# A 256-token model of two hybrid blocks on one core: seven of the 32 weight pieces of each first-block mixer have their low parts subtracted by GpSimd

## What is computed

```python
for l in range(DEPTH):                       # first block, DEPTH = 2
    h = rms_norm(x, ffn1_norm[l])
    x = x + 0.5 * swiglu(h, ffn1_w_gate[l], ffn1_w_up[l], ffn1_w_down[l])
    h = rms_norm(x, mix_norm[l])
    (na_q, ..., dl_v) = split_in_proj(h @ w_in[l])
    o_a = neighborhood_attention(...); o_b = diff_attention(...)
    o_c = gqa_axial_attention(...);    o_d = dilated_attention(...)
    x = x + jnp.concatenate([o_a, o_b, o_c, o_d], axis=-1) @ w_out[l]
    h = rms_norm(x, ffn2_norm[l])
    x = x + 0.5 * swiglu(h, ffn2_w_gate[l], ffn2_w_up[l], ffn2_w_down[l])
...
for l in range(DEPTH):                       # second block
    h = rmsnorm(x, g_mix_pre[l]) * (1.0 + scale_a) + shift_a
    y = hybrid_mixer(h, ...)
    x = x + gate_a * rmsnorm(y, g_mix_post[l])
    h = rmsnorm(x, g_ffn_pre[l]) * (1.0 + scale_f) + shift_f
    x = x + gate_f * rmsnorm(swiglu_2(h, w_gate_up[l], w_down[l]), g_ffn_post[l])
```

## Time and profile before

| what | value |
|---|---|
| median of 3 runs | 1707.03 us (1704.61 to 1708.94) |
| the profiled execution, its own time | 1706.23 us |
| its span, first to last instruction | 1704.4 us |
| TensorE busy | 1633.8 us (96%), 8104 matmuls |
| VectorE busy | 1194.8 us (70%), 1833 instructions |
| ScalarE busy | 932.1 us (55%), 1789 instructions |
| GpSimd busy | 92.0 us (5%), 155 instructions |
| VectorE `Wl<-raw,Wh` (L1644) | 316 of 1.204 us |
| VectorE `QTl<-raw,QTh` (L1644) | 178 of 1.208 us |

### The profile page before, as it was taken

How to read it: one execution, slowest core, us unless ns; L and a number is a source line. 1 busy time by engine, 2 the same in 40 slices (tenths; PEclk the granted TensorE clock), 3 DMA queues, 4 the chain that set the end, 5 groups by cost and what they waited for, 6 DMA issues and landing times.

```text
span 1704.4 us, 22248 instructions
## 1 busy us (share of the span) xinstructions
PE 1633.8 (96%) x8104; PEld 1354.8 (79%) x8104; DVE 1194.8 (70%) x1833; ACT 932.1 (55%) x1789; POOL 92.0 (5%) x155
## 2 busy tenths in 40 slices
PE   7999998899999999998899999989999989899998
PEld 6888877788888888877788887778788878778887
DVE  6877689777776777769787776767645476675554
ACT  6445568654445444557754445757534467664342
POOL 0000112100000000022000000101000010010000
PEclk9999999999999999999999999999999999999999
DMA  8787634277866887634177784523665642346551
GB/s 315 265 296 257 218 112 136 87 266 253 278 231 204 276 279 253 241 100 143 50 243 275 254 275 135 176 99 95 219 201 176 182 156 82 112 139 222 197 182 63
DMA packets 100107, 329.87 MB, mean 194 GB/s; under 512 B 18800, under 2 KB 19312, under 8 KB 99488
## 3 DMA queue, kind: packets, MB, share of 16 engines
q1 hardware_dynamic: 85504, 276.59, 48.4%
q10 hardware_dynamic: 14496, 51.87, 9.2%
HBM read 327.32 MB, written 1.10 MB: 193 GB/s over the span
## 4 chain that ended last, share of the span: by engine, by line
PE 45%; DVE 6%; ACT 3%; issue 1%; POOL 1%; DVEq 0%; POOLq 0%; ACTq 0%
PE PS L819 14%; PE PS L821 14%; PE PS L820 14%; PE PS L973 1%; PE PS L885 1%; DVE Wl L1644 1%; DVE PTl L1840 1%; PE PS L993 1%; DVE st L1809 1%; ACT WK L1368 1%; DVE QTl L1644 0%; DVE WK L1806 0%; PE PS L1150 0%; ACT Wh L1252 0%; ACT WK L1379 0%
## 5 line engine op out<-in xcount | busy, mean ns | idle before, releaser
L1644 DVE TENSOR_TENSOR Wl<-raw,Wh 128x1024 fp32r<-128x1024 f32 (+1 forms) x316 | 371.0, 1204 | 44.9 <-ACT Wh L1252 44.0
L819 PE MATMUL PS<-Wh,Hh 128*128 128x512 f32 (+2 forms) x936 | 370.2, 396 | 9.5 <-DVE Hl L1707 3.5
L820 PE MATMUL PS<-Wl,Hh 128*128 128x512 f32 (+2 forms) x936 | 365.0, 390 | 0.0
L821 PE MATMUL PS<-Wh,Hl 128*128 128x512 f32 (+2 forms) x936 | 364.9, 390 | 0.0
L1252 ACT ACTIVATE Wh<-raw 128x1024 fp32r<-128x1024 f32 (+1 forms) x316 | 317.4, 1041 | 25.8 <-DVE PTl L1755 11.0
L1644 DVE TENSOR_TENSOR QTl<-raw,QTh 128x1024 fp32r<-128x1024 f32 (+2 forms) x178 | 211.5, 1208 | 19.8 <-ACT QTh L1252 19.6
L819 PEld LDWEIGHTS PS<-Wh,Hh 128*128 128x128 f32 x936 | 178.2, 190 | 48.9 <-DVE WK L1740 3.9
L821 PEld LDWEIGHTS PS<-Wh,Hl 128*128 128x128 f32 x936 | 178.2, 190 | 36.4
L820 PEld LDWEIGHTS PS<-Wl,Hh 128*128 128x128 f32 x936 | 178.3, 191 | 33.9
L819 PE MATMUL PS<-QTh,Hh 128*128 128x512 f32 (+2 forms) x504 | 196.5, 390 | 3.8 <-DVE Hl L1707 3.8
L821 PE MATMUL PS<-QTh,Hl 128*128 128x512 f32 (+2 forms) x504 | 194.9, 387 | 0.0
(11 more groups left out here) (232 smaller groups left out, 2525.0 us busy)
## 6 DMA issues: line engine op xcount, KB each, us to landing
raw<-in_ffn SPq DMA_DIRECT2D x396, 512.0 KB, 5.3
BT<-in_ada ACTq DMA_DIRECT2D x96, 512.0 KB, 4.5
raw<-in_win SPq DMA_DIRECT2D x64, 512.0 KB, 4.5
raw<-in_wo SPq DMA_DIRECT2D x32, 512.0 KB, 4.5
...
```

The lines of the kernel that those rows point to most:

```text
L819: e.matmul(out_, xh, wh, start=start, stop=False)
L820: e.matmul(out_, xh, wl, start=False, stop=False)
L821: return e.matmul(out_, xl, wh, start=False, stop=stop)
L1644: ins = e.tensor_tensor(low(p)[:, 0:w], raw[p % RAW][:, 0:w], high(p)[:, 0:w].bitcast(f32), ALU.subtract)
```

## The change

GpSimd takes the low parts of pieces 10, 13, 16, 19, 22, 25 and 28 of each stage `a`; VectorE leaves them out. They are counted on a semaphore of their own, `w_low_pool`; `w_lo` counts the rest. Whoever waited for `w_lo` of a piece now calls `wait_low`. The events of both kinds of mixer are in a new order on TensorE, ScalarE and VectorE, and GpSimd's list of stage `a` has `parts` events. Second-block mixers have no piece on GpSimd; only their lists are changed.

```diff
+POOL_PIECES = (10, 13, 16, 19, 22, 25, 28)
...
             "PE": [("proj", 0, 0, 0), mid[0], mid[1], ("proj", 1, 0, 0), ("proj", 0, 1, 0), ("proj", 1, 1, 0),
                 ("proj", 2, 0, 0), ("turn_qk", 0, 0, 0), ("proj", 2, 1, 0), ("S", 0, 0, 0), ("turn_qk", 1, 0, 0),
                 ("proj", 3, 0, 0), ("S", 1, 0, 0), ("T", 0, 0, 0), ("S", 2, 0, 0), ("proj", 3, 1, 0), ("V", 0, 0, 0),
-                ("T", 1, 0, 0), ("S", 3, 0, 0), ("proj", 4, 0, 0), ("T", 2, 0, 0), ("V", 1, 0, 0), ("proj", 4, 1, 0),
-                ("turn_qk", 2, 0, 0), ("V", 2, 0, 0), ("S", 4, 0, 0), ("proj", 5, 0, 0), ("T", 3, 0, 0), ("S", 5, 0, 0),
+                ("S", 3, 0, 0), ("T", 1, 0, 0), ("proj", 4, 0, 0), ("V", 1, 0, 0), ("T", 2, 0, 0), ("proj", 4, 1, 0),
+                ("turn_qk", 2, 0, 0), ("V", 2, 0, 0), ("proj", 5, 0, 0), ("S", 4, 0, 0), ("T", 3, 0, 0), ("S", 5, 0, 0),
...
-            "ACT": [("proj", 0, 0, 0), ("parts", 8, 0, 0), mid[0], mid[1], ("parts", 9, 0, 0), ("proj", 1, 0, 0),
-                ("parts", 11, 0, 0), ("parts", 12, 0, 0), ("proj", 0, 1, 0), ("parts", 14, 0, 0), ("norm", 0, 0, 0),
+            "ACT": [("proj", 0, 0, 0), ("parts", 8, 0, 0), mid[0], ("parts", 8, 0, 0), ("parts", 10, 0, 0), mid[1],
+                ("proj", 1, 0, 0), ("parts", 13, 0, 0), ("proj", 0, 1, 0), ("norm", 0, 0, 0), ("parts", 14, 0, 0),
                 ("proj", 1, 1, 0), ("norm", 1, 0, 0), ("proj", 2, 0, 0), ("turn_qk", 0, 0, 0), ("proj", 2, 1, 0),
...
-            "DVE": [("parts", 7, 0, 0), ("parts", 8, 0, 0), mid[0], mid[1], ("proj", 0, 1, 0), ("parts", 9, 0, 0),
-                ("parts", 13, 0, 0), ("norm", 0, 0, 0), ("rope", 0, 0, 0), ("norm", 1, 0, 0), ("proj", 2, 0, 0),
...
+            "DVE": [("parts", 5, 0, 0), ("parts", 8, 0, 0), mid[0], ("parts", 8, 0, 0), mid[1], ("parts", 13, 0, 0),
+                ("proj", 0, 1, 0), ("norm", 0, 0, 0), ("rope", 0, 0, 0), ("norm", 1, 0, 0), ("proj", 2, 0, 0),
+                ("parts", 13, 0, 0), ("turn_qk", 0, 0, 0), ("rope", 1, 0, 0), ("proj", 2, 1, 0), ("S", 0, 0, 0),
+                ("parts", 16, 0, 0), ("turn_qk", 1, 0, 0), ("N", 0, 0, 0), ("proj", 3, 0, 0), ("S", 1, 0, 0), ("T", 0, 0, 0),
+                ("parts", 18, 0, 0), ("parts", 20, 0, 0), ("S", 2, 0, 0), ("N", 1, 0, 0), ("proj", 3, 1, 0),
...
-            "POOL": [("norm", 0, 0, 0), ("norm", 1, 0, 0), ("norm", 2, 0, 0), ("norm", 3, 0, 0), ("sums", 0, 0, 0),
-                ("sums", 1, 0, 0), ("res", s, 0, 0), ("res", s, 1, 0)],
+            "POOL": [("parts", 11, 0, 0), ("norm", 0, 0, 0), ("norm", 1, 0, 0), ("parts", 17, 0, 0), ("norm", 2, 0, 0),
+                ("parts", 20, 0, 0), ("parts", 14, 0, 0), ("parts", 23, 0, 0), ("norm", 3, 0, 0), ("parts", 26, 0, 0),
+                ("parts", 29, 0, 0), ("sums", 0, 0, 0), ("sums", 1, 0, 0), ("res", s, 0, 0), ("res", s, 1, 0)],
...
+        w_low_pool = semaphore("w_low_pool")
...
+        on_pool = [first["a", l] + x for l in range(L) for x in POOL_PIECES]
+
+        def low_parts(p):
+
+            return parts(p) - sum(x <= p for x in on_pool)
+
+        def wait_low(e, p):
+
+            if p in on_pool:
+                e.wait_ge(w_low_pool, on_pool.index(p) + 1)
+            else:
+                e.wait_ge(w_lo, low_parts(p))
...
                 if p >= RAW:
-                    e.wait_ge(w_lo, parts(p - RAW))
+                    wait_low(e, p - RAW)
                 e.dma_start(raw[p % RAW][:, 0:w], src).then_inc(raw_in[p % RAW], 16)
...
                 while state["lo"] < dve_weights[s, i]:
                     p = state["lo"]
+                    state["lo"] += 1
+                    if p in on_pool:
+                        continue
...
+            def low_piece():
+                p = on_pool[state["low"]]
+                w = pieces[p][1]
+                e.wait_ge(w_hi, parts(p))
+                e.tensor_tensor(low(p)[:, 0:w], raw[p % RAW][:, 0:w], high(p)[:, 0:w].bitcast(f32), ALU.subtract
+                                ).then_inc(w_low_pool, 1)
+                state["low"] += 1
...
+                    elif what == "parts":
+                        while state["low"] < len(on_pool) and on_pool[state["low"]] < min(first[stage] + x, first[stage] + 32):
+                            low_piece()
```

More of the change, by code:

```diff
@@ L132, in walk @@
                 ("wo", (6, 7), 0, 0), ("sums", 1, 0, 0), ("wo", (3,), 1, 0), nxt[0], ("wo", (4,), 1, 0), ("rows", 1, 0, 0),
-                ("wo", (5,), 1, 0), nxt[1], ("wo", (6, 7), 1, 0)],
-            "ACT": [("proj", 0, 0, 0), ("parts", 8, 0, 0), mid[0], mid[1], ("parts", 9, 0, 0), ("proj", 1, 0, 0),
-                ("parts", 11, 0, 0), ("parts", 12, 0, 0), ("proj", 0, 1, 0), ("parts", 14, 0, 0), ("norm", 0, 0, 0),
+                nxt[1], ("wo", (5,), 1, 0), ("wo", (6, 7), 1, 0)],
+            "ACT": [("proj", 0, 0, 0), ("parts", 8, 0, 0), mid[0], ("parts", 8, 0, 0), ("parts", 10, 0, 0), mid[1],
+                ("proj", 1, 0, 0), ("parts", 13, 0, 0), ("proj", 0, 1, 0), ("norm", 0, 0, 0), ("parts", 14, 0, 0),
@@ L136, in walk @@
                 ("proj", 1, 1, 0), ("norm", 1, 0, 0), ("proj", 2, 0, 0), ("turn_qk", 0, 0, 0), ("proj", 2, 1, 0),
[L137 to L140, removed]
@@ L141, in walk @@
-                ("turn_qk", 2, 0, 0), ("proj", 4, 1, 0), ("parts", 28, 0, 0), ("norm", 3, 0, 0), ("V", 2, 0, 0),
[6 rows of a table removed]
-                ("rows", 0, 0, 0), ("parts", 35, 0, 0), ("V", 9, 0, 0), ("sums", 1, 0, 0), ("parts", 37, 0, 0),
-                ("res", s, 0, 0), nxt[0], ("rows", 1, 0, 0), nxt[1], ("parts", 37, 0, 0), ("res", s, 1, 0),
-                ("parts", 39, 0, 0)],
-            "DVE": [("parts", 7, 0, 0), ("parts", 8, 0, 0), mid[0], mid[1], ("proj", 0, 1, 0), ("parts", 9, 0, 0),
-                ("parts", 13, 0, 0), ("norm", 0, 0, 0), ("rope", 0, 0, 0), ("norm", 1, 0, 0), ("proj", 2, 0, 0),
-                ("turn_qk", 0, 0, 0), ("rope", 1, 0, 0), ("parts", 14, 0, 0), ("proj", 2, 1, 0), ("S", 0, 0, 0),
-                ("parts", 17, 0, 0), ("N", 0, 0, 0), ("turn_qk", 1, 0, 0), ("proj", 3, 0, 0), ("S", 1, 0, 0),
[3 rows of a table removed]
-                ("turn_qk", 2, 0, 0), ("parts", 27, 0, 0), ("parts", 28, 0, 0), ("norm", 3, 0, 0), ("S", 4, 0, 0),
[6 rows of a table removed]
+                ("parts", 17, 0, 0), ("turn_qk", 1, 0, 0), ("E", 0, 0, 0), ("proj", 3, 0, 0), ("N", 0, 0, 0),
@@ new lines, in walk @@
+                ("parts", 18, 0, 0), ("parts", 18, 0, 0), ("T", 0, 0, 0), ("E", 1, 0, 0), ("parts", 21, 0, 0),
+                ("proj", 3, 1, 0), ("norm", 2, 0, 0), ("N", 1, 0, 0), ("V", 0, 0, 0), ("E", 2, 0, 0), ("T", 1, 0, 0),
+                ("N", 2, 0, 0), ("proj", 4, 0, 0), ("E", 3, 0, 0), ("T", 2, 0, 0), ("V", 1, 0, 0), ("parts", 25, 0, 0),
+                ("parts", 26, 0, 0), ("proj", 4, 1, 0), ("turn_qk", 2, 0, 0), ("parts", 28, 0, 0), ("parts", 28, 0, 0),
[6 rows of a table added]
+                ("rows", 0, 0, 0), ("parts", 33, 0, 0), ("V", 9, 0, 0), ("parts", 35, 0, 0), ("sums", 1, 0, 0),
@@ new lines, in walk @@
+                ("parts", 37, 0, 0), ("res", s, 0, 0), nxt[0], ("rows", 1, 0, 0), nxt[1], ("res", s, 1, 0),
+                ("parts", 37, 0, 0), ("parts", 39, 0, 0)],
+            "DVE": [("parts", 5, 0, 0), ("parts", 8, 0, 0), mid[0], ("parts", 8, 0, 0), mid[1], ("parts", 13, 0, 0),
[3 more added lines that the diff above has]
+                ("parts", 18, 0, 0), ("parts", 20, 0, 0), ("S", 2, 0, 0), ("N", 1, 0, 0), ("proj", 3, 1, 0),
+                ("parts", 20, 0, 0), ("norm", 2, 0, 0), ("S", 3, 0, 0), ("N", 2, 0, 0), ("T", 1, 0, 0), ("V", 0, 0, 0),
+                ("rope", 2, 0, 0), ("parts", 21, 0, 0), ("T", 2, 0, 0), ("V", 1, 0, 0), ("parts", 25, 0, 0), ("N", 3, 0, 0),
+                ("parts", 25, 0, 0), ("turn_qk", 2, 0, 0), ("parts", 28, 0, 0), ("norm", 3, 0, 0), ("V", 2, 0, 0),
[6 rows of a table added]
@@ L165, in walk @@
                 ("V", 9, 0, 0), ("res", s, 0, 0), ("sums", 1, 0, 0), ("parts", 35, 0, 0), ("rows", 1, 0, 0),
-                ("parts", 36, 0, 0), nxt[0], nxt[1], ("res", s, 1, 0), ("parts", 37, 0, 0), ("parts", 39, 0, 0)],
-            "POOL": [("norm", 0, 0, 0), ("norm", 1, 0, 0), ("norm", 2, 0, 0), ("norm", 3, 0, 0), ("sums", 0, 0, 0),
-                ("sums", 1, 0, 0), ("res", s, 0, 0), ("res", s, 1, 0)],
+                ("parts", 35, 0, 0), nxt[0], nxt[1], ("res", s, 1, 0), ("parts", 37, 0, 0), ("parts", 39, 0, 0)],
@@ L178, in walk @@
                 ("T", 4, 0, 0), ("O", 2, 0, 0), ("wo", (1,), 0, 0), ("S", 6, 0, 0), ("V", 4, 0, 0), ("T", 5, 0, 0),
[3 rows of a table removed]
[L182 to L187, removed]
[7 rows of a table removed]
[3 rows of a table added]
@@ new lines, in walk @@
+                ("wo", (2,), 1, 0), ("wo", (3,), 1, 0), ("wo", (4,), 1, 0), nxt[0], ("wo", (5,), 1, 0), ("wo", (6, 7), 1, 0),
+                nxt[1]],
+            "ACT": [("parts", 9, 0, 0), mid[0], mid[1], ("proj", 0, 0, 0), ("proj", 1, 0, 0), ("parts", 9, 0, 0),
```

(27 more changed lines are left out.)

## The result

The changed kernel takes 1716.84 us in the median (1712.73 to 1724.41, 9 runs) against 1708.94 us before (1704.61 to 1710.73, 9 runs). The ratio is 1.0052 with a 95% interval of 1.004 to 1.0063: slower by some 9 us. The forecast was 3 us slower, 1710, in a range of 1697 to 1723; the measured time lies in the range, but above the 1705 to 1713 that the forecast called its own.

What follows compares the result with a forecast made beforehand. VectorE's queue was taken to bound the dense stretch of first-block mixers. 8.7 us blocked against 6.35 saved per mixer left VectorE 4.7 later in both, times 0.7 +3.3 on 1706.2: 1709.5, 1710 as median; range 1697 to 1723.

Steps and rivals of the forecast that it cites:

- GpSimd's duration: GpSimd's subtractions in first-block mixers: 2.7 us per 1024-column piece, 1.4 for the narrow one, 17.6 for seven.
- Turns: VectorE operations with two SBUF inputs and GpSimd's alternate by instruction; those reading PSUM don't wait.
- The places: Blocking per first-block mixer, piece by piece: 13 2.6 us, 16 2.7, 19 0, 22 1.4, 25 2.0, 28 0; sum 8.7.
- The signs: Profile after: VectorE busy 1 to 5 us more, its two-input operations about 17 us longer; under 50 of 60 refutes.
- one factor of 0.7: Share of a VectorE delay in the dense stretch passed to the end: 4.7 us in both mixers gives +3.3.
- The lists: Reordered events of the second-block mixers: given nothing, between -2 and +2 us, as VectorE is a third idle there.
- Rival 3: The edits do nothing, softmax chain bounds the dense stretch, new lists cost what they bring: 1707 us; chance 0.10.
- Rival 1: Waiting hardly bites in the first-block mixers, a piece costs VectorE under 0.46 us: 8.9 off, 1698 us; chance 0.25.
- rival 2: Every first-block piece blocks in full or costs more, from 1.7 us per piece: 1724 us, or 1719 with 0.7; chance 0.25.
- New waits for `raw`: New ScalarE waits for raw buffers would refute the forecast; piece 31's later reload was to stay hidden by 3.4 us.

Runs made afterwards that it cites:

- run 8: Changed kernel, but GpSimd copies the raw piece (one input) in place of subtracting the high part: 1704.14 us, 0.9975.
- runs 9 to 11: On one chip, second block's new lists alone: 1699.75 us; with five gated GpSimd pieces added: 1698.1 us; those with only their first column subtracted: 1698.3 us.
- run 3: Changed kernel, but GpSimd subtracts only the first column of each of its pieces, the rest left out: 1698.22 us, 0.994.
- run 7: Changed kernel with each GpSimd piece as four instructions of a quarter of the columns: 1711.72 us, 1.0024.
- run 1: Changed kernel with all new lists but no piece on GpSimd, VectorE subtracting all 32: 1706.91 us, 0.9995.
- runs 2 and 6: Seven pieces, old TensorE, ScalarE and VectorE lists: 1725.18 us, 1.0096; five ungated pieces, old first-block and new second-block lists: 1715.8 us, 1.0049.
- run 4: Kernel before with the new lists in the second block's mixers alone: 1701.4 us, 0.9958.
- run 5: Old first-block, new second-block lists; GpSimd takes five pieces, each held by a gate until VectorE comes to PSUM work: 1699.45 us, 0.9946.
- run 10: The kernel with five gated GpSimd pieces, old first-block and new second-block lists, measured again: 1698.1 us, 0.9946.

## Why the prediction held, and where it was off

**Direction and range** held, and so did the mechanism: GpSimd's pieces and VectorE's two-input work take turns, and that costs more than the relief brings. The size was off: +3.3 us forecast, some +9 measured. (Of the 7 us between 1710 and 1716.84, 2 are the base: the runs of the kernel before had 1707.03 in the median then and 1708.94 now.)

**GpSimd's duration.** 2.7 us from the rope tables' slope; measured 2.40 where nobody was ahead of it (3.32 with a wait for VectorE), 1.50 for the narrow piece. The Trainium skill, "GPSIMD Engine Reference", section 3.1, has 4497 ns for 2048 columns, halved an estimate of 2.25 us. The measurement lies between the two.

**Turns.** That VectorE's operations with two inputs in SBUF and GpSimd's subtractions exclude each other, and PSUM readers do not, is shown: by the profile after, by the gate (0.0 against 14.6 us of excess for the same five pieces) and by the quarters. The Trainium skill, "SBUF — State Buffer", section "Who interferes with whom", says that the second one blocks until the first is finished. This holds for the subtraction (L1926 at 233.71 ends 1.08 us behind GpSimd's piece, and alone takes 1.23). It doesn't for GpSimd's one-input instruction, which lets VectorE go long before its end (run 8), nor for the 5.43 us power in the earlier trace rows. That GpSimd shuts VectorE out only while it reads its inputs would fit both; no run measured it by itself.

**The places.** I expected 8.7 us of excess per mixer and found 10.5 in a0 and 8.5 in a1. The sum was nearly right and its terms were not: that they made up for each other is luck. Piece 13 isn't beside `norm 0`'s chain, since GpSimd's `parts 11` covers piece 10 alone; it stands behind the root of `norm 1` and met that group's L1926 (2.2 us in both mixers, where I had 2.6). Piece 19 stands behind the root of `norm 2` and cost 1.4 in place of 0. Piece 22 cost 0 in place of 1.4. Piece 28 was right behind 25 and cost 2.0 in place of 0. Piece 25 cost 1.8 where I took 2.0, and 16 cost 2.1 and 1.0 where I took 2.7. Piece 10 cost 0.95 in a0 (I had 0) and 0 in a1.

**The signs.** VectorE's busy time was to be 1 to 5 us above before's: 4.2. Its two-input operations were to be longer by 17 us: 18.9. It was to stay over 50 us busy in 60 of the dense stretch: 54.3 and 55.9.

**The step that failed** is the last one: one factor of 0.7 for gains and losses alike, put on their difference. The runs give a factor to each. The work taken away (15 us) gave back 9 on the new lists, 0.6, and most of that only made good what these lists cost; on the old ones it was under 0.2 (runs 9 to 11). The excess counted in full. Above run 3, on the same lists, run 8 has 5.9 us of excess and 6 us of time, run 7 15.6 and 14, the change 18.9 and 19. With these the sum is 18.9 - 9.4 = +9.5 for the pieces, measured +10. In group 3 the reason is seen: GpSimd's pieces stood right behind the root, held up the operations that TensorE was about to need, and the excess came back as TensorE's wait (3.8 us of each). For the other groups I take it to be the same; it wasn't traced wait by wait.

**The lists** were to give nothing. They gave two things that nearly cancel: -0.42% in the second block, +0.37% in the first. Rival 3's "lists made anew cost as much as they bring" was true of the two parts together, but not of the change. That the lists could be left out of the sum was luck as well. Rival 1 (hardly bites) is out; rival 2 put the blocking at 14.9 us a mixer, but a piece costs nothing where VectorE reads PSUM. By rival 2's own measure, which shares the blocking among six pieces, the 9.5 us found per mixer are 1.6 us a piece: the forecast had 1.4, rival 2 begins at 1.7. It was close.

**New waits for `raw`** were named as a sign against the forecast, and there are two, short ones. Who waited for whom, ScalarE, 205 to 352 and 720 to 878 us:

```profile
ACT Wh L1270 <- DMA raw<-in_wo: 1.3, 1, 1.3
...
ACT Wh L1270 <- DMA raw<-in_wo: 1.0, 1, 1.0
```

The trace before has none there. The pieces are not the cause: run 1, with none on GpSimd, has them with 1.1 us each, and runs 2 and 6, with whole pieces on the old lists, have none. They come with the new lists of the first block (run 3 has 1.5 and 1.3 us), though not always: runs 7 and 8, on these lists but on another chip than runs 1 and 3, have none. What they cost was not measured.

**Open.** The kernel of run 4 changes nothing ahead of stage b0. Yet its traces, in both runs, have a1 at 136.5 us where before's has 138.9, at a granted clock of 0.97 against 0.95; b0 and b1 together gained 3.1, and f4 and f5 some 0.9. So of the 7 us only about 4 lie where the edit is or behind it. Of the kernel before there is one trace, and traces of one kernel differ as well: a0 takes 131.4 us in run 5 and 132.9 in run 10, b1 131.5 and 129.8. Whether the kernel or the execution makes the difference in a1 is not shown. It bears on the size of the lists' effects, not on that of the pieces, where time and excess agree.
